# First score maps of attention within the last projection chunk, a narrower low operand, and column sums as one product of ones

## The reference

```python
def rms_norm(x, g):
    y = xf * lax.rsqrt(jnp.mean(xf * xf, axis=-1, keepdims=True) + NORM_EPS)
...
    h = rms_norm(x, g_mix) * (1 + scale1) + shift1
    mo, k, v = mixer(h, w_in_l, lambda_l, subln_l, conv_l, w_out_l, lam_init, k_ctx, v_ctx)
    x = x + gate1 * mo
    h = rms_norm(x, g_ffn) * (1 + scale2) + shift2
    x = x + gate2 * ffn(h)
...
        s = jnp.einsum('bqhsd,bkhsd->bshqk', qblk, k).astype(jnp.float32) * scale
        p = jax.nn.softmax(s, axis=-1)
        a = p[:, 0] - lam * p[:, 1]
        return jnp.einsum('bhqk,bkhe->bqhe', a.astype(v.dtype), v)
```

## Time and profile before

| what | value |
|---|---|
| median of 3 runs | 1975.42 us (1972.21 to 1979.14) |
| profiled execution, own time | 1974.79 us |
| its span in the trace | 1972.9 us |
| TensorE busy | 1910.0 us, 97% |
| VectorE, ScalarE, GpSimd busy | 57%, 41%, 6% |
| mean granted clock of TensorE | 0.99 |

### The profile page before, as it was taken

How to read it: one execution, slowest core, us unless ns; L and a number is a source line. 1 busy time by engine, 2 the same in 40 slices (tenths; PEclk the granted TensorE clock), 3 DMA queues, 4 the chain that set the end, 5 groups by cost and what they waited for, 6 DMA issues and landing times.

```text
span 1972.9 us, 30669 instructions
## 1 busy us (share of the span) xinstructions
PE 1910.0 (97%) x12579; PEld 1748.1 (89%) x12579; DVE 1117.6 (57%) x1799; ACT 803.2 (41%) x1331; POOL 122.2 (6%) x102
## 2 busy tenths in 40 slices
PE   8999889999999999999999899899999999999997
PEld 6999768999999999999997588899898988989885
DVE  2643776444332344437347754476676766768577
ACT  4221364322211222222213644455565655656564
POOL 2000000100000000110000001220000000002210
PEclk8999999999999999999998999899999999999999
DMA  9525100324231431305252011577686776768762
GB/s 348 183 79 205 62 1 22 108 97 181 76 118 43 176 124 65 124 27 192 81 199 53 1 44 39 144 231 244 218 250 212 223 241 204 246 201 303 256 196 73
DMA packets 91699, 290.49 MB, mean 147 GB/s; under 512 B 13236, under 2 KB 21812, under 8 KB 91552
## 3 DMA queue, kind: packets, MB, share of 16 engines
q1 hardware_dynamic: 84416, 270.15, 41.2%
q0 software_dynamic: 7136, 18.30, 2.9%
HBM read 281.98 MB, written 12.28 MB: 149 GB/s over the span
## 4 chain that ended last, share of the span: by engine, by line
PE 90%; DVE 5%; ACT 2%; issue 2%; DMA 1%; SPq 0%; DVEq 0%; ACTq 0%
PE ps L706 47%; PE ps L1056 12%; PE ps L1045 12%; PE ps L1046 6%; PE ps L766 2%; PE ps L891 2%; PE ps L1049 2%; PE ps L882 1%; DVE pr L1995 1%; DVE nbias L1971 1%; PE ps L1048 1%; PE ps L739 1%; DMA ada_raw<-ada_w 1%; PE ps L898 1%; PE ps L1120 1%
## 5 line engine op out<-in xcount | busy, mean ns | idle before, releaser
L1734 DVE TENSOR_TENSOR w_lo<-raw,w_hi 128x1024 fp32r<-128x1024 f32 x394 | 485.2, 1233 | 385.4 <-ACT w_hi L1226 375.7
L1226 ACT ACTIVATE w_hi<-raw 128x1024 fp32r<-128x1024 f32 x394 | 414.4, 1053 | 343.4 <-PE ps L706 172.3
L1045 PE MATMUL ps<-hg,w_hi 128*128 128x416 f32 x1232 | 380.7, 366 | 2.0 <-DVE hg L2152 1.8
L706 PE MATMUL ps<-a_hi,w_hi 128*128 128x320 f32 x1472 | 343.3, 314 | 3.4 <-DVE a_lo L1776 3.4
L706 PE MATMUL ps<-a_lo,w_hi 128*128 128x320 f32 x1472 | 341.0, 313 | 0.0
L706 PE MATMUL ps<-a_hi,w_lo 128*128 128x320 f32 x1472 | 339.9, 312 | 0.0
L1046 PE MATMUL ps<-hg,w_lo 128*128 128x208 f32 x1232 | 319.9, 260 | 0.0
L706 PEld LDWEIGHTS ps<-a_hi,w_hi 128*128 128x128 f32 x1472 | 249.8, 191 | 11.2 <-issue 7.4
L706 PEld LDWEIGHTS ps<-a_hi,w_lo 128*128 128x128 f32 x1472 | 250.9, 190 | 0.0
L706 PEld LDWEIGHTS ps<-a_lo,w_hi 128*128 128x128 f32 x1472 | 250.1, 190 | 0.0
L1045 PEld LDWEIGHTS ps<-hg,w_hi 128*128 128x128 f32 x1232 | 232.8, 189 | 4.3 <-DVE hg L2152 2.0
(11 more groups left out here) (257 smaller groups left out, 2439.3 us busy)
## 6 DMA issues: line engine op xcount, KB each, us to landing
raw<-gu_w SPq DMA_DIRECT2D x220, 512.0 KB
raw<-moe_down_w SPq DMA_DIRECT2D x88, 512.0 KB
ada_raw<-ada_w SPq DMA_DIRECT2D x21, 2048.0 KB, 8.1
raw<-in_w SPq DMA_DIRECT2D x48, 512.0 KB
raw<-down_w SPq DMA_DIRECT2D x22, 512.0 KB
raw<-out_w SPq DMA_DIRECT2D x16, 512.0 KB
ada_pro<-ada_w SPq DMA_DIRECT2D x2, 2048.0 KB, 19.1
y_rows<-ey POOLq DMA_DIRECT2D x7, 512.0 KB
```

What stands on the lines that cost most here:

```text
L706: ins = nc.tensor.matmul(out[:, hf, 0:c1 - c0], w, o[:, c0:c1], start=f, stop=e)
L1045: nc.tensor.matmul(sums, whi, both, start=(k == 0), stop=False)
L1226: nc.scalar.activation(w_hi[:, s, :], raw[:, n % RAW, :], ACT.Copy).then_inc(hi_done, 1)
L1734: nc.vector.tensor_tensor(w_lo[:, s, :], raw[:, n % RAW, :], w_hi[:, s, :].bitcast(F32), ALU.subtract)\
```

## The change

- `TA` is 644, and `a_lo` has only the 640 token columns: the shift's low part now stands as two more columns of `a_hi`. Products with `a_hi` have 324 columns in the second half instead of 322, those with `a_lo` 320. `scaled` adds the pairs by a reduction, and where it also scales (the four q chunks) a second small operation follows.
- The norms i = 1 and 2: GpSimd adds all eight squares; `norm_total` at tile 4 multiplies them by ones, so that the sum stands in every partition; ScalarE's root goes over 640 columns straight into `rstd` (`keep_root`), and VectorE takes the reciprocal of 640 columns in `free_spread`. The one-column products, the diagonal and the spreading are gone there; i = 0 and 3 stay.
- The block numbers of `"in"` are padded (`IN_PAD`), so that its last chunk lies in block 3 of PSUM. By `plan()` the pad is 2 in layer 0 (`"in"` now starts at 7) and 0 in layer 1. VectorE adds the pad to `blk_free` in `free_spread`.
- Scores of maps 0 and 1 now stand ahead of the last chunk, those of map 2 at its tile 4. Their maxima stand on VectorE ahead of the last chunk's `scaled`.

```diff
-TA = T + 2
+TA = T + 4
...
-        steps += [("norm1", 0, 2 * l, l), ("in", chunks, len(items), len(items)),
-                 ("sub", 0, HEADS, None), ("out", OUT_CH, OUT_CH, OUT_CH), ("norm2", 0, 2, 1)]
+        steps += [("norm1", 0, l, l), ("in", chunks, len(items), len(items)),
+                 ("sub", 0, HEADS, None), ("out", OUT_CH, OUT_CH, OUT_CH), ("norm2", 0, 1 + l, 1)]
...
+            if name == "in":
+
+                IN_PAD[l] = (3 - (g + len(items) - 1)) % 4
+                g += IN_PAD[l]
...
-            a_lo = sb("a_lo", [P, KB, TA], F32R, c=ops)
+            a_lo = sb("a_lo", [P, KB, T], F32R, c=ops)
...
-                        c0, c1 = (0, HALF) if hf == 0 else (HALF, width)
+                        c0, c1 = (0, HALF) if hf == 0 else (HALF, T if o is opnd_lo else width)
                         ins = nc.tensor.matmul(out[:, hf, 0:c1 - c0], w, o[:, c0:c1], start=f, stop=e)
...
+            def norm_total(i):
+
+                g0 = NORM_AT[i][2]
+                open_block(g0)
+                pe.wait_ge(ss_add, KB * (i + 1))
+                for hf in range(2):
+                    ins = nc.tensor.matmul(ps[:, g0 % 4, hf, 0:HALF], ones[:], ss[:, hf * HALF:(hf + 1) * HALF],
+                                           start=True, stop=True)
+                ins.then_inc(mm_done, 1)
...
-                    if norm_i is not None and k == 2:
-                        norm_sums(norm_i)
-                    if norm_i is not None and k == 5:
-                        norm_spread(norm_i)
+                    if norm_i is not None and k == 4:
+                        norm_total(norm_i)
...
+                in_blocks = g0 + len(IN_SEQ[l])
...
+                    if b == len(IN_SEQ[l]) - 1:
+
+                        if l == 0:
+                            pe.wait_ge(late_in, 16 * 9)
+                        pe.wait_ge(kq_ready, 8 * (l + 1))
+                        pe.wait_ge(cache_in[l], 32)
+                        pe.wait_ge(blk_free, in_blocks - 2)
+                        scores(0, 1)
...
+                            if b == len(IN_SEQ[l]) - 1 and k == 4:
+
+                                pe.wait_ge(blk_free, in_blocks - 1)
+                                scores(2)
...
-                if l == 0:
-                    pe.wait_ge(late_in, 16 * 9)
-
-
-                pe.wait_ge(blk_free, g0 + len(IN_SEQ[l]))
-                pe.wait_ge(kq_ready, 8 * (l + 1))
-                pe.wait_ge(cache_in[l], 32)
                 pe.wait_ge(vtok_ready, 4 * (l + 1))
...
-                scores(0, 1)
-                scores(2)
                 for i, (h, t, k0, nk) in enumerate(STEPS):
                     scores(2 * i + 3, 2 * i + 4)
+                    if i == 0:
+
+                        pe.wait_ge(blk_free, in_blocks)
...
+            def keep_root(i):
+
+                n0, q0, g0 = NORM_AT[i]
+                act.wait_ge(mm_done, q0 + 1)
+                nc.scalar.activation(rstd, ps[:, g0 % 4, :, 0:HALF], ACT.Sqrt, bias=eps[:, 0:1], scale=1.0 / D)\
+                    .then_inc(rstd_ready, 1)
...
-                    root(2 * l, D)
-                    keep_rstd(2 * l)
+                    keep_root(2 * l)
...
-                act.wait_ge(mm_done, AT[l, "sub"][1])
+                act.wait_ge(mm_done, q0 + IN_SEQ[l].index(("turn", 3)) + 1)
...
-                root(2 * l + 1, D)
                 if l == 0:
-                    keep_rstd(1)
+                    keep_root(1)
                 else:
+                    root(3, D)
                     modulate()
 
...
-                    elif kb == KB - 1:
+                    elif kb == KB - 1 and i in (0, 3):
 
                         pool.wait_ge(ss_add, m)
...
-                    nc.vector.tensor_tensor(a_lo[:, :, T:TA], mods[:, l, 3 * which * KB:(3 * which + 1) * KB, :],
-                                            a_hi[:, :, T:TA].bitcast(F32), ALU.subtract)
+                    nc.vector.tensor_tensor(a_hi[:, :, T + 2:TA], mods[:, l, 3 * which * KB:(3 * which + 1) * KB, :],
+                                            a_hi[:, :, T:T + 2].bitcast(F32), ALU.subtract)
...
             def free_spread(i):
 
                 dve.wait_ge(rstd_ready, i + 1)
-                dve.sem_inc(blk_free, 1)
+                dve.sem_inc(blk_free, 1 + (IN_PAD[i // 2] if i % 2 == 0 else 0))
+                if i:
+                    link(nc.vector.reciprocal(ss[:], ss[:]))
...
-                nc.vector.tensor_scalar(bcol[:, col, :], ps[:, slot, 1, HALF:HALF + 2], scale, None, ALU.mult)
+                parts = ps[:, slot, 1, HALF:HALF + TA - T].rearrange("p (h c) -> p c h", c=2)
+                if scale == 1.0:
+                    nc.vector.tensor_reduce(bcol[:, col, :], parts, AX, ALU.add)
+                else:
+                    link(nc.vector.tensor_reduce(bcol[:, col, :], parts, AX, ALU.add))
+                    nc.vector.tensor_scalar(bcol[:, col, :], bcol[:, col, :], scale, None, ALU.mult)
                 return nc.vector.tensor_tensor(halves(dst), ps[:, slot, :, 0:HALF], rstd, ALU.mult)
...
-                    reciprocal_root(2)
...
+                        if j == CONV_BLOCKS - 1:
+                            for m in range(3):
+                                row_max(m)
                         dve.wait_ge(mm_done, q0 + b + 1)
                         scaled(tt[:, 1, :], slot, c % 8).then_inc(in_scaled, 1)
                         dve.wait_ge(in_scaled, done)
...
-                for m in range(3):
-                    row_max(m)
...
-                    reciprocal_root(1)
```

More of the change, by code:

```diff
@@ L205 @@
 DENSE_BLOCKS = blocks_of(DENSE)
-PAD = {}
+PAD, IN_PAD = {}, {}
 def plan():
@@ L403, in hybrid_step @@
         ht_hi = a_hi[:].rearrange("p a b -> p (a b)")[:, 0:T * KB].rearrange("p (t d) -> p t d", t=TT)
-        ht_lo = a_lo[:].rearrange("p a b -> p (a b)")[:, 0:T * KB].rearrange("p (t d) -> p t d", t=TT)
+        ht_lo = a_lo[:].rearrange("p a b -> p (a b)").rearrange("p (t d) -> p t d", t=TT)
         rstd = ss[:].rearrange("p (a b) -> p a b", a=2)
@@ L754, in norm_spread @@
                     fill(NORM_AT[i][2] + 1, FILL["spread"])
-                pe.wait_ge(diag_ready, i + 1)
+                pe.wait_ge(diag_ready, 2 if i else 1)
                 spread(NORM_AT[i][2], diag[:].rearrange("p t c -> p (t c)"))
@@ L885, in scores @@
                             ins.then_inc(scores_done if m % 2 else scores_even, 1)
+                n0, q0, g0 = AT[l, "in"]
+                in_blocks = g0 + len(IN_SEQ[l])
+                two_blocks([(n0, g0), (n0 + 1, g0 + 1)], operand[l, "h1"], 2 * l if l else None)
+                for b, (item, c) in enumerate(IN_ITEMS[l][0]):
+                    if b < 2:
+                        continue
+                    kind, j = item[0], item[1]
+                    if kind == "ada":
+                        if item[1] == "turn":
+                            turn_rows(g0 + b, item[2] + 1)
+                        else:
+                            open_block(g0 + b)
+                            pe.wait_ge(ada_full, 16 * (u + 1))
+                            weigh_conditions(ada_raw, g0 + b, item[3], True, True)
+                            u += 1
+                        continue
+                    if b == len(IN_SEQ[l]) - 1:
[5 more added lines that the diff above has]
+                        scores(0, 1)
+                    if kind != "turn":
+                        pe.wait_ge(lo_done, n0 + c + 1)
+                    open_block(g0 + b)
+                    if kind == "turn":
+                        pe.wait_ge(vt_ready, 4 * l + j + 1)
+                        for t in range(TT):
+                            ins = nc.tensor.transpose(ps[:, (g0 + b) % 4, t // 4, (t % 4) * P:(t % 4 + 1) * P],
+                                                      vT[:, j, t * P:(t + 1) * P], idn[:])
+                    else:
+                        for k in range(KB):
+                            if b == len(IN_SEQ[l]) - 1 and k == 4:
+                                pe.wait_ge(blk_free, in_blocks - 1)
+                                scores(2)
+                            ins = product(ps[:, (g0 + b) % 4], ((n0 + c) % SPLIT, k), a_hi[:, k, :], a_lo[:, k, :],
+                                          k == 0, k == KB - 1, TA)
+                    ins.then_inc(mm_done, 1)
+                pe.wait_ge(vtok_ready, 4 * (l + 1))
                 def weigh_values(i):
@@ L1255, in gained @@
                     act.wait_ge(mod_ready, i + 1)
-                    nc.scalar.activation(a_hi[:, :, T:TA], mods[:, l, 3 * which * KB:(3 * which + 1) * KB, :], ACT.Copy)
+                    nc.scalar.activation(a_hi[:, :, T:T + 2], mods[:, l, 3 * which * KB:(3 * which + 1) * KB, :], ACT.Copy)
                 if i:
@@ L1298, in _ @@
                     take_rows(0, g0)
-                    keep_rstd(0)
+                    keep_rstd()
                     act.wait_ge(mm_done, q0 + ADA_FIRST.index(("turn", 0, 0)) + 1)
@@ L1741, in reciprocal_root @@
```

(9 more changed lines are left out.)

44 lines of the change are left out of this document (5 added, 39 removed).

## The result

The changed kernel takes 1962.45 us (median of 5 runs, 1959.82 to 1971.29), the kernel before, run beside it, 1978.22 us (5 runs, 1972.21 to 1979.95): ratio 0.9939, 95% interval 0.9920 to 0.9959. It is faster by 0.6%, some 12 us where 3.9 were forecast, and its median lies under the predicted range.

What follows compares the result with a forecast made beforehand. The prediction took TensorE, busy 97% of the span, as the bound. Its terms, 7.45 + 0.35 - 4.24 - 3.4 - 1.7 - 1.1 - 1.3 = -3.9 us, gave a 1971.5 us median; range 1966.5 to 1977.5.

Steps and rivals of the forecast that it cites:

- the term for the columns: Projection chunks: `a_lo` pairs falling to 320 columns gain 2.9 us, wider `a_hi` pairs cost 1.2; -1.7 us.
- 148.6 ns a matmul named as a sign: Time per matmul in the projection chunks that the later profile would show if the forecast was right.
- The wait at the start: Layer 0's projection: TensorE idles until 49.8 for a fifth freed block, +7.45 us, then +0.35 us for a lower clock.
- the fifth comes only from `free_spread(0)`: Layer 0's start: the fifth freed block comes behind all `a_lo` tiles and the third chunk's `split_lo`, at 49.75.
- The norms: Norms 1 and 2: one-column sums leave, -4.24 us, and the clock no longer falls behind them, -3.4 us.
- The 3.9 to 6.2 us for the reciprocal: VectorE's reciprocal of 640 columns, by two slopes from smaller sizes; hidden by the third chunk, so 0 us.
- the slower rival: Reciprocal becomes the bound ahead of the first scaling, from 6.9 us on; at 12 us, 1981.7 us; chance 0.04.
- The estimate of 5.3 us: Reciprocal of 640 columns on VectorE, from a divide step repeated 8 times at 0.96 GHz; under 6.9 us.
- Start of attention: Last chunk of either layer: earlier scores and maxima bring the fourth maximum 0.53 us earlier; two layers, -1.1 us.
- Clock in attention: Start of attention: denser TensorE work may avoid one layer's lower clock, 2.65 us; half counted, -1.3 us.
- They are early enough: Start of attention: exponentials waiting for `newv`, landing 4.5 to 5.5 us after issue, suffice for a mixing near 234.6.
- the rival of the absent wait: Layer 0's start: a fifth block is freed before TensorE asks, so 7.8 us fall away; 1963.7 us, chance 0.05.

Runs made afterwards that it cites:

- x10_lo_width: Kernel before with 320 instead of 322 columns in products with `a_lo`, all addresses kept; 192 records took 28.65 us.
- x9_lo_pitch: Changed kernel with rows of `a_lo` 644 numbers apart instead of 640, columns kept; 192 records took 28.45 us.
- x5_pitch: Kernel before with rows of `a_hi` and `a_lo` 644 numbers apart instead of 642, products unchanged; ratio 0.9975, 192 records 28.48 us.
- x14_weights_moved: Changed kernel with 128 bytes left free behind the operands, so `w_hi` and `w_lo` lie later; 192 records took 28.40 us.
- x15_lo_moved: Changed kernel with 128 bytes left free between `a_hi` and `a_lo`, so `a_lo` and the weights lie later; 192 records took 28.45 us.
- x4_free: Changed kernel with the norm's block and the pad of layer 0 freed ahead of the operand's tiles; 1959.18 us, ratio 0.9913.
- x2_norms: Kernel before with the norm part alone (`norm_total`, `keep_root`, the reciprocal in `free_spread`); 1969.78 us, ratio 0.9971.
- x8_after_again: The changed kernel run once more, nothing altered; 1962.41 us, ratio 0.9943.
- x1_cols: Kernel before with the column part alone (`TA` 644, `a_lo` without extra columns, and what reads them); ratio 0.9949.
- x7_stores: x4_free with SyncE issuing the stores newk and newv ahead of the loads of `out_w`; 1957.72 us, ratio 0.9913.
- x12_no_scores: Kernel before with column part and norm part, without padded numbers and moved scores; 1956.84 us, ratio 0.9906.
- x13_stores_only: x12_no_scores with the stores newk and newv issued ahead of the loads of `out_w`; 1958.43 us, ratio 0.9917.
- x6_widths: x4_free with `a_hi` rows 648 numbers apart and second-half columns rotating over 320 to 328; pairs with `a_hi` took 293.4 to 297.1 ns.
- x7_again: x7_stores run once more, beside x13_stores_only; 1957.24 us, ratio 0.9911.

## Why the prediction was wrong

**What failed is the term for the columns.** "At the granted 2.4 GHz two columns are 0.83 ns: +1.2, which I take, as clock cycles they must cost at least": -1.7 us, with -2.9 as the best case; it is -9.2. The two rates of the earlier trace rows were right, but I put the whole 3.9 ns a pair down to the columns, as they were the difference that the diff showed; the 320-column row reads other buffers (`ca_`, `cc_`), too. x10_lo_width against before, and x9_lo_pitch against x5_pitch, show that the columns make next to nothing; x5_pitch, x14_weights_moved and x15_lo_moved that the addresses do. The diff changed the rows of both operands and the start of `a_lo`, by `TA` and the shape of `a_lo`, and left the weights in place. (The 148.6 ns a matmul named as a sign belong to -2.9 us; -1.7 us would be 148.9.)

The formula N / 2.4 + 2.5 ns that the prediction took from the Trainium skill's page "TensorE: Matmul & The Clock Gate" ("Back-to-back issue gap") counts columns only; the trace does not agree, as the same columns took 28.26 to 28.45 us. That page of the Trainium skill itself gives the formula for single, isolated matmuls, and says that in a stream the load of weights and the matmul set the spacing together. x14_weights_moved, slower by its weights' place, fits that. Which addresses are good, and whether the load or the matmul is slowed, stays open.

**The wait at the start: right in kind, too long.** 7.45 us of wait and 0.35 of clock were forecast. The wait is 4.33 us; with 5.46 us at 0.50 behind it A grows by 6.2. From start to start, the second chunk follows the first product after 6.30 us instead of 1.30, so 5.0 us are the wait's and 1.2 the clock's. The step "the fifth comes only from `free_spread(0)`, and that stands on VectorE behind ... `split_lo` of the third chunk" is wrong in its second half: the operation needed that `w_lo` to be let in (46.88), not to be done (49.47), so the wait is shorter by 2.4 us; another 0.7 us is that the trace counts it only from the modelled end of the six matmuls (42.76). x4_free shows cause and price: 5.5 us back by freeing the block a few lines earlier.

**The norms: right.** -3.82 us each were forecast; x2_norms has -3.73 and -3.72, the changed kernel -3.88 with the columns' 0.1. In both places the clock stayed. The 3.9 to 6.2 us for the reciprocal hold (4.15 us), and so does that it is hidden, so the slower rival had no ground. The estimate of 5.3 us from the Trainium skill's page "VectorE: DVE Perf Modes" ("First, the fixed hardware budget") is 1.15 us too long; the lower slope of the earlier trace rows was nearer.

**Start of attention: the step was right, its sum not.** The forecast -0.53 us a layer took 1.6 us for three maps. In layer 1 maps 0 and 1 take from 1043.32 to the next product's start at 1043.74, and the last chunk with map 2 inside grows by 1.7 us (map 2 from 1047.48 to 1048.96 and the restart behind it). Rows of the changed kernel:

```profile
1043.32 0.49 PE L855 MATMUL ps<-kT,qT 64*128 64x128 f32 x4
1043.74 0.58 PE L710 MATMUL ps<-a_hi,w_hi 128*128 128x320 f32 x2
...
1047.48 1.55 PE L855 MATMUL ps<-kT,qT 64*128 64x512 f32 x4
1048.96 0.56 PE L710 MATMUL ps<-a_hi,w_hi 128*128 128x320 f32 x2
```

So it is 0.5 + 1.7 = 2.2 us, 0.6 more than forecast, and that is the forecast's gain: in layer 0, both without the low clock, B + F is 249.49 before and 247.24 after, of which 2.2 is stage B's and 0.1 the last chunk's columns.

**Clock in attention: its size fits, its cause is not shown.** -1.3 us were forecast. In layer 0 the low clock came in five of the table's six executions with the scores moved, and in three of five without; in layer 1 G is 85.5 to 86.5 us with them and 88.1 to 88.3 in three of four without, where the landing was quick. x2_norms with 86.06 us and unmoved scores speaks against a rule. Without x2_norms layer 1 has 2.0 us less in G and 0.5 more ahead of it, some -1.4 us, which the times can't tell from nothing.

**What no term had: the landing of `newv`.** "They are early enough" holds for landings up to 5.6 us (x14_weights_moved), where the fourth maximum of layer 1 starts 12.39 us behind the last chunk's first product. With 6.8 us (x8_after_again) it starts at 13.55, 1.2 us late. With 9.1 and 11.0 us G takes 90.3 and 91.8, without the moved scores (x1_cols) and with them (after), so it explains the first profiled execution's small gain and not the change's worth.

With what was measured the sum is +6.2 - 2 x 3.72 - 9.2 + 0 - 1.4 = -11.8 us, or -10.4 if the clock in attention counts for nothing; the ratio says -12.1 (-8.1 to -15.8), which fits both. The forecast's error is thus the columns' 7.5 us, then the start's 1.6; the rival of the absent wait (1963.7 us) gave the right time for a wrong reason.

## What to carry to other kernels

When a diff changes a buffer's shape, it changes addresses too, of its rows and often of the buffers behind it: cost it as a change of placement with a bound of its own, and test shape and placement apart, by a kernel that has only the padding. A padded count is only as harmless as the place at which the missing credit is given: look for where it could be given earlier, since that was worth 5.5 us here. Of x4_free, x7_stores, x12_no_scores and x13_stores_only, all near ratio 0.991, none can be told from the others, so the simplest, x12_no_scores, is the one to keep: the moved scores bring nothing measurable, and cost 6 us where they force a wait.

## What the runs showed of the hardware

- Products of 128x128 fp32r weights over two halves of 320 and 320 to 324 columns took 147.2 to 149.3 ns a matmul by where operands and weights lay. 128 bytes more between operands and weights made 28.26 us into 28.40 for 192 records, while products whose operands moved along kept 44.18 to 44.20 us for 300.
- Two columns less in a third of the products took 28.65 us where it had been 28.66 (x10_lo_width); a pair of halves with `a_hi` took 293.4 ns with 320 and 296.1 with 328 columns in the second half (x6_widths).
- A semaphore operation in VectorE's queue released TensorE at 47.09 us, 0.21 behind the end of the `w_hi` (46.88) that the `w_lo` ahead of it waits for, while this `w_lo` began only at 48.26.
- VectorE's reciprocal of 640 columns took 4.15 us, 6.5 ns a column.
- The same store of 256 KB landed 4.2 us after its issue in one execution (x2_norms) and 11.0 us in another (after). Issued ahead of the loads of `out_w` it took 11.1 to 11.9 us (x7_stores, x7_again, x13_stores_only). Why was not found.
- Three maps of scores lengthened TensorE's path by 2.2 us when they stood ahead of and within a chunk, and took 1.75 us with their modelled end when they stood behind it.
